# Hybrid decoder layer: the depthwise convolution as three filters by parity of tokens, its norm's sums in float32r of rounded values and rests

## The reference, cut to what matters

```python
u = conv_val * jax.nn.sigmoid(conv_gate)
u = causal_depthwise_conv(u, conv_w[layer], conv_b[layer])      # width 31, 512 channels
uf = u.astype(jnp.float32).reshape(B, S, N_CONV_GROUPS, CONV_GROUP_DIM)   # 4 groups of 128
mu_c = jnp.mean(uf, axis=-1, keepdims=True)
var_c = jnp.mean(jnp.square(uf - mu_c), axis=-1, keepdims=True)
uf = ((uf - mu_c) * lax.rsqrt(var_c + EPS)).reshape(B, S, D_CONV)
uf = uf * conv_norm_w[layer].astype(jnp.float32) + conv_norm_b[layer].astype(jnp.float32)
y_conv = jax.nn.silu(uf).astype(x.dtype)
```

## Time and profile before

| | |
|---|---|
| time, median of 3 runs | 2086.36 us (2085.43 to 2087.7) |
| the profiled execution's own time | 2085.33 us |
| its span, first to last instruction | 2083.5 us |
| TensorE busy | 2067.1 us (99%) |
| VectorE busy | 1446.1 us (69%) |
| ScalarE busy | 912.1 us (44%) |
| mean granted TensorE clock | 0.998 |

### The profile page before, as it was taken

The page is one execution under the profiler, slowest core; times in us unless marked ns, Lnnn a source line. Parts: engine busy times, 40 slices in busy tenths (PEclk is TensorE's granted clock), DMA queues, the critical chain, the costliest instruction groups (busy, mean ns, idle before and its releaser), DMA issues. The chain is left out here.

```text
span 2083.5 us, 26901 instructions
## 1 busy us (share of the span) xinstructions
PE 2067.1 (99%) x10031; PEld 1734.2 (83%) x10031; DVE 1446.1 (69%) x1993; ACT 912.1 (44%) x1557; POOL 417.2 (20%) x252
## 2 busy tenths in 40 slices
PE   9999999999999999999999999999999999999998
PEld 8897878878788888788888888888788888888887
DVE  6897999989567777886666976666563536624285
ACT  6632434343454445754555654455331313313163
POOL 0000000000002323352332333232353134400012
PEclk9999999999999999999999999999999999999999
DMA  5121212113656875765446755545756455543376
GB/s 204 32 87 47 70 41 81 51 32 105 199 177 195 266 235 171 266 192 167 137 142 191 236 171 156 167 150 189 245 210 259 154 193 202 174 169 126 138 257 218
DMA packets 254144, 338.55 MB, mean 162 GB/s; under 512 B 11584, under 2 KB 195648, under 8 KB 240192
## 3 DMA queue, kind: packets, MB, share of 16 engines
q1 hardware_dynamic: 221376, 315.80, 45.6%
q10 hardware_dynamic: 32384, 20.98, 3.2%
q0 software_dynamic: 256, 0.07, 0.0%
HBM read 225.58 MB, written 111.21 MB: 162 GB/s over the span
## 5 line engine op out<-in xcount | busy, mean ns | idle before, releaser
L1978 PE MATMUL psum<-x_hi,w_hi_P 128*128 128x512 f32 x896 | 349.8, 390 | 3.8 <-DVE x_lo L1922 2.4
L2198 PE MATMUL psum<-w_hi,hid_hi 128*128 128x512 f32 x896 | 348.8, 389 | 1.9 <-DVE hid_lo L2074 1.9
L1978 PE MATMUL psum<-x_lo,w_hi_P 128*128 128x512 f32 x896 | 349.1, 390 | 0.0
L1978 PE MATMUL psum<-x_hi,w_lo_P 128*128 128x512 f32 x896 | 349.1, 390 | 0.0
L2198 PE MATMUL psum<-w_hi,hid_lo 128*128 128x512 f32 x896 | 348.6, 389 | 0.0
L2198 PE MATMUL psum<-w_lo,hid_hi 128*128 128x512 f32 x896 | 348.6, 389 | 0.0
L2074 DVE TENSOR_TENSOR hid_lo<-hid_raw,hid_hi 128x1024 fp32r<-128x1024 f32 x112 | 174.4, 1593 | 211.4 <-ACT hid_hi L2069 211.4
L1891 POOL TENSOR_TENSOR w_raw<-w_raw 128x512 f32<-128x512 f32 x128 | 184.9, 1467 | 395.3 <-DVE w_lo_P L1904 345.8
L2069 ACT ACTIVATE hid_hi<-hid_raw 128x1024 fp32r<-128x1024 f32 x112 | 112.9, 1051 | 343.4 <-DMA hid_raw<-scratch_hid 343.3
L1904 DVE TENSOR_TENSOR w_lo_P<-w_raw,w_hi_P 128x512 fp32r<-128x512 f32 x224 | 184.1, 834 | 98.1 <-ACT w_hi_P L1900 95.5
L1900 ACT ACTIVATE w_hi_P<-w_raw 128x512 fp32r<-128x512 f32 x224 | 136.0, 626 | 236.8 <-PE psum L1978 227.2
(11 more groups left out here) (284 smaller groups left out, 3820.0 us busy)
## 6 DMA issues: line engine op xcount, KB each, us to landing
scratch_hid<-stage SPq DMA_DIRECT2D x224, 256.0 KB, 3.7
hid_raw<-scratch_hid SPq DMA_DIRECT2D x56, 1024.0 KB, 4.9
w_raw<-in_w SPq DMA_DIRECT2D x52, 1024.0 KB, 5.0
w_grain<-in_w SPq DMA_DIRECT2D x48, 512.0 KB, 5.3
x_raw<-scratch_h2s SPq DMA_DIRECT2D x14, 1024.0 KB, 8.4
w_raw<-in_w_in SPq DMA_DIRECT2D x22, 512.0 KB, 3.6
scratch_h2s<-h2s SPq DMA_DIRECT2D x8, 1280.0 KB, 10.1
scratch_qk<-qout ACTq DMA_DIRECT2D x16, 512.0 KB, 3.3
```

Of the source, the lines that this page charges most:

```text
L1978: mm = nc.tensor.matmul(psum[:, bank_1(op, g), :], l, r, start=kt == 0 and i == 0, stop=kt == 3 and i == 2)
L2198: mm = nc.tensor.matmul(psum[:, bank, :], l, r, start=f == 0 and k == 0, stop=f == NFP - 1 and k == 2)
```

## The change

Tokens are stored by parity: `u_buf` holds a unit's even and odd tokens in two halves, each with its own head. Three filters of half the length run over 512 or 513 pairs each: A (the 16 even taps over the one half), B (the 15 odd taps over the other), and M (sums of neighbouring taps over sums of neighbouring tokens, `u_pairs`). Even outputs are A + B, odd ones are M minus (A shifted + B). A unit is `N_STEPS` = 48 steps on VectorE: S (the token sums), 15 A, 14 B, 15 M, E, T and O. ScalarE makes the first product of each filter (`first_taps`, `pair_tap`), and in its loop these stand ahead of `silu_qk` and `first_tap_qk`. `SILU` puts the tokens back in order as it writes.

For the norm, ScalarE rounds `c_buf` to float32r (`HIGH`), VectorE makes the rest (`LOW`), and the sums are float32r matmuls of both; the squares are treated alike (`HIGH` of the square on ScalarE, `SQUARE_LOW` on VectorE). The rounded values lie in the unit's own place in `u_buf`, so `glu` of the unit that comes to that place now waits for all six counts of `ln_sum`, that is for `VAR` and no longer for the last tap.

```diff
-AT_MEAN, AT_CENTER, AT_SQUARE, AT_VAR, AT_RSTD, AT_NORM, AT_SILU = 1, 2, 3, 4, 5, 6, 7
-LAST_UNIT_AT = {AT_MEAN: 0, AT_CENTER: 0, AT_SQUARE: 0, AT_VAR: 1, AT_RSTD: 1, AT_NORM: 1, AT_SILU: 1}
+UNIT_AT = {AT_HIGH: 0, AT_SUM_HIGH: 1, AT_LOW: 1, AT_SUM_LOW: 2, AT_CENTER: 2, AT_SQUARE: 3, AT_SQUARE_LOW: 3,
+           AT_VAR: 5, AT_RSTD: 6, AT_NORM: 7, AT_SILU: 8}
+LAST_UNIT_AT = {AT_HIGH: 0, AT_SUM_HIGH: 1, AT_LOW: 1, AT_SUM_LOW: 2, AT_CENTER: 2, AT_SQUARE: 2, AT_SQUARE_LOW: 2,
+                AT_VAR: 3, AT_RSTD: 3, AT_NORM: 3, AT_SILU: 3}
-TAP_COST = 23
+STEP_COST = 12.6
...
+def unit_steps():
+    out = [("S", 0)]
+    for j in range(1, EVEN):
+        out += [("A", j)] + ([("B", j)] if j < ODD else []) + ([("M", j - 1)] if j > 1 else [])
+    return out + [("E", 0), ("M", EVEN - 1), ("T", 0), ("O", 0)]
...
-                    for b in range(2):
-                        group_sum(c_buf[:, u % 2], b)
+                    for b in range(2):
+                        group_sum(high_part(u), b, True, False).then_inc(sem["ln_sum"], 1)
+                for u in units_at(s, AT_SUM_LOW):
+                    pe.wait_ge(sem["ln_dve"], 3 * u + 1)
+                    for b in range(2):
+                        group_sum(high_part(u), b, False, True).then_inc(sem["ln_sum"], 1)
                 for u in units_at(s, AT_VAR):
-                    pe.wait_ge(sem["c_sq"], u + 1)
+                    pe.wait_ge(sem["ln_act"], 3 * u + 3)
+                    pe.wait_ge(sem["ln_dve"], 3 * u + 3)
                     for b in range(2):
-                        group_sum(rstd, b)
+                        group_sum(high_part(u), b, True, False)
+                        group_sum(square_low, b, False, True).then_inc(sem["ln_sum"], 1)
...
+                for u in units_at(s, AT_HIGH):
+                    act.wait_ge(sem["tap"], step_done(u, "O"))
+                    nc.scalar.activation(high_part(u), c_buf[:, u % 2], ACT.Copy).then_inc(sem["ln_act"], 1)
...
+                for u in range(N_UNITS):
+                    if FIRST_TAP[u] == s:
+                        first_taps(u)
+                    if PAIR_TAP[u] == s:
+                        pair_tap(u)
                 for j, half in convs_at(s - 2):
                     silu_qk(j, half)
                 for j, half in convs_at(s):
                     first_tap_qk(j, half)
-                for u in range(N_UNITS):
-                    if FIRST_TAP[u] == s:
-                        first_tap(u)
-                    if SECOND_TAP[u] == s:
-                        second_tap(u)
...
                 if tb % 2 == 0 and u >= U_RING:
-                    dve.wait_ge(sem["tap"], DVE_TAPS * (u - U_RING + 1))
+                    dve.wait_ge(sem["ln_sum"], LN_SUMS * (u - U_RING + 1))
...
+                nc.vector.scalar_tensor_tensor(out=a_sum, in0=u_halves(u)[:, 0, j:j + UH + 1],
+                                               scalar=par[:, CONV_W + g * CW + 2 * j:CONV_W + g * CW + 2 * j + 1],
+                                               in1=a_sum, op0=ALU.mult, op1=ALU.add).then_inc(sem["tap"], 1)
...
                 for j, half in convs_at(s - 1):
                     convolve_qk(j, half)
+                for u in units_at(s, AT_LOW):
+                    dve.wait_ge(sem["ln_sum"], LN_SUMS * u + 2)
+                    nc.vector.tensor_tensor(high_part(u), c_buf[:, u % 2], high_part(u).bitcast(F32),
+                                            ALU.subtract).then_inc(sem["ln_dve"], 1)
...
+                for u in units_at(s, AT_SQUARE_LOW):
+                    dve.wait_ge(sem["ln_act"], 3 * u + 3)
+                    nc.vector.tensor_tensor(square_low[:], rstd[:], high_part(u).bitcast(F32),
+                                            ALU.subtract).then_inc(sem["ln_dve"], 1)
```

More of the change, by code:

```diff
@@ L498, in slot, with group_sum @@
                 mm.then_inc(sem["proj"], 1)
-            def group_sum(src, b):
-                nc.tensor.matmul(psum[:, 6 + b, :], ones[:], src[:, b * TB:(b + 1) * TB],
-                                 start=True, stop=True).then_inc(sem["ln_sum"], 1)
+            def group_sum(src, b, start, stop):
+                return nc.tensor.matmul(psum[:, 6 + b, :], ones_r[:], src[:, b * TB:(b + 1) * TB], start=start, stop=stop)
             scores, numerators, transpose_y = tail["tensor"](pe)[:3]
@@ L513, in tensor @@
                 slot(s)
-                for u in units_at(s, AT_MEAN):
-                    pe.wait_ge(sem["tap"], DVE_TAPS * (u + 1))
+                for u in units_at(s, AT_SUM_HIGH):
+                    pe.wait_ge(sem["ln_act"], 3 * u + 1)
                     if u == 0:
@@ new lines, in odd_tap @@
+            def odd_tap(u, j):
+                g = u // 2
+                if j == 1:
+                    dve.wait_ge(sem["tap0"], 3 * u + 2)
+                else:
+                    dve.wait_ge(sem["tap"], step_done(u, "B", j - 1))
+                nc.vector.scalar_tensor_tensor(out=b_sum, in0=u_halves(u)[:, 1, j:j + UH],
+                                               scalar=par[:, CONV_W + g * CW + 2 * j + 1:CONV_W + g * CW + 2 * j + 2],
+                                               in1=b_sum, op0=ALU.mult, op1=ALU.add).then_inc(sem["tap"], 1)
@@ new lines, in even_tokens, with both_sums, odd_tokens @@
+            def even_tokens(u):
+                dve.wait_ge(sem["tap"], step_done(u, "A", EVEN - 1))
+                nc.vector.tensor_tensor(c_buf[:, u % 2, 0:UH], a_sum[:, 0:UH], b_sum, ALU.add).then_inc(sem["tap"], 1)
+            def both_sums(u):
+                dve.wait_ge(sem["tap"], step_done(u, "E"))
+                nc.vector.tensor_tensor(b_sum, a_sum[:, 1:UH + 1], b_sum, ALU.add).then_inc(sem["tap"], 1)
+            def odd_tokens(u):
+                dve.wait_ge(sem["tap"], step_done(u, "T"))
+                nc.vector.tensor_tensor(m_sum(u), m_sum(u), b_sum, ALU.subtract).then_inc(sem["tap"], 1)
@@ new lines, in conv_step @@
+            def conv_step(n):
+                u = n // N_STEPS
+                kind, j = STEPS[n % N_STEPS]
+                if kind == "S":
+                    add_pairs(u)
+                elif kind == "A":
+                    even_tap(u, j)
+                elif kind == "B":
+                    odd_tap(u, j)
+                elif kind == "M":
+                    pair_tap(u, j)
+                elif kind == "E":
+                    even_tokens(u)
+                elif kind == "T":
+                    both_sums(u)
+                else:
+                    odd_tokens(u)
@@ new lines, in add_weights @@
+            def add_weights():
+                taps = par[:, CONV_W:CONV_W + H * CW].rearrange("p (g k) -> p g k", g=H)
+                sums = pairs[:, 0:H * EVEN].rearrange("p (g j) -> p g j", g=H)
+                nc.vector.tensor_tensor(sums[:, :, 0:ODD], taps[:, :, 0:CW - 1:2], taps[:, :, 1:CW - 1:2], ALU.add)
+                nc.vector.tensor_copy(sums[:, :, ODD:EVEN], taps[:, :, CW - 1:CW])
+                link(nc.vector.tensor_scalar(pairs[:, H * EVEN:H * EVEN + H], par[:, CONV_B:CONV_B + H], 2.0, None, ALU.mult))
```

165 lines of the change are left out of this document (107 added, 58 removed).

## The result

The changed kernel takes **2104.36 us** (median of 4 runs, 2103.3 to 2107.08) against 2086.56 for the kernel before (2085.43 to 2087.7): ratio 1.0088, 95% interval 1.0076 to 1.01. It is slower by 17.8 us; I had forecast slower by 7. The profiled execution took 2103.3.

The account below looks back on a forecast made before the run. TensorE was taken as the bound, busy 2067.1 of 2083.5 us. Terms -13.1 - 1.9 + 0.7 + 2.7 + 0.7 + 6.4 + 8.0 + 3.4 = +6.9 gave 2092.2 profiled, 2093 forecast, range 2080 to 2098.

Parts of the forecast that it names:

- main case: Long TensorE pauses both at unit 6 and at the tail: slower, 2093 us, own range 2089 to 2097; chance 0.52.
- Sums, -13.1: On TensorE, eight float32r matmuls a unit replace two pairs of float32 sums: -13.1 us over eight units.
- waits that go, -1.9: TensorE's waits for the convolution's mean (1.1 us) and slot 91's wait for an evacuation (0.78) vanish: -1.9 us.
- VectorE at 0.66 us a step: On VectorE, each filter step over 512 tokens takes 0.66 us, 48 steps making 31.7 us a unit.
- rival (5): VectorE's steps cost more than 0.66 us (0.74), so deadlines are missed in each unit: 2103 us; chance 0.08.
- Units 2, 3 and 6: TensorE waits for HIGH or LOW at these units: +0.7, +2.7 (0.9 and 1.8), and +0.7 with +6.4 us.
- Units 0, 1, 4 and 5 ... nothing there: HIGH of these units has 1 to 5 us left before TensorE needs it, so no wait was charged.
- The chain behind VAR is the same. +8.0: At the tail, TensorE waits for yc_c at scores(0), only slot 91 lying between: +8.0 us, bounds 6.5 and 8.5.
- I charge each the same: +3.4: Half clock on TensorE behind the 6.4 and 8.0 us pauses, 1.7 us lost each: +3.4 us, bounds 0 and 6.
- (2): Only the tail pause comes, LOW of unit 6 waiting for little: 2085 us; chance 0.17.
- (3): Only unit 6's pause comes, yc_c no longer being last: 2088 us at best, 2083 if all goes; chance 0.1.
- (4): Neither the pause at unit 6 nor that at the tail comes: 2075 us, faster; chance 0.13.

Follow-up runs that it names:

- last mended kernel: The four edits of the mended kernels, plus eight of unit 7's steps in VectorE's slot 80 with LOW of unit 6 ahead of them: 2077.91 us.
- mended kernels: Changed kernel with LOW ahead of q/k block, slot 55's silu ahead of RSTD, own buffer for unit 6's tokens, float32 sums for unit 7: 2085.97 us.
- hand-made pause of 7.96 us: Kernel before, with TensorE's means of units 4 and 5 made to wait for three and six more taps: 2099.13 us, 1.0061.
- loads by half: Changed kernel with own buffers for tokens of units 6 and 7, first eight chunks' yc_c loads waiting only for first-half units: 2101.41 us, 1.0069.

## Why the prediction was wrong in size

The sign and the main case (pauses at unit 6 and at the tail) were right. The forecast for the profiled execution was 2092.2; it took 2103.3, 11.1 more. By its terms:

- **Sums, -13.1, and waits that go, -1.9:** held as far as seen: the sum for the last mended kernel comes out with 11.4 for seven units and 1.1 of the waits, and the 0.78 at slot 91 is gone from the changed kernel's waits (it is back where unit 7's sums are float32).
- **VectorE at 0.66 us a step:** held. VectorE's timeline around a glu, and the later glu that waits for VAR of unit 2:

```profile
271.54 0.68 DVE L902 SCALAR_TENSOR_TENSOR u_buf<-th,psum 128x512 f32<-128x512 f32 x1
272.14 0.75 DVE L933 SCALAR_TENSOR_TENSOR c_buf<-u_pairs,pair_weights,c_buf 128x512 f32<-128x512 f32 x1
272.80 0.75 DVE L912 SCALAR_TENSOR_TENSOR ab_buf<-u_buf,par_a,ab_buf 128x513 f32<-128x513 f32 x1
...
289.72 0.18 DVE L895 COPY u_buf<-u_buf 128x30 f32<-128x30 f32 x1 [7.47 <-PE psum L556]
```

  Steps start 0.66 apart, and `glu` with strides takes 0.68 as before, so nothing was the right price for it and rival (5), steps above 0.70, is out.
- **Units 2, 3 and 6:** forecast 0.7, 0.9 + 1.8, 0.7 + 6.4; measured 0.76, 0.91 + 1.85, 1.04 + 5.88. (The terms written out for unit 2 add to 9.5, not 9.7, which makes its wait 0.5.) The glu of slot 45 waits 7.47 us for VAR of unit 2, as said. LOW ahead of the block showed that the q/k block was the cause.
- **"Units 0, 1, 4 and 5 ... nothing there": wrong for unit 4**, 3.25. I counted steps and left out ScalarE's order: RSTD one slot later meets the silu of block (5, 0). Shown by the move of that silu, in slot 55 alone in the mended kernels: the wait for HIGH is 0.50 there. A wait of 1.27 for LOW then shows, so even with the silu in place "nothing there" was 1.8 us short. That part was not tested; as at unit 2, VectorE has S, seven steps and here a weight split too (1.14) between O and LOW.
- **"The chain behind VAR is the same. +8.0": mis-sized, 9.55 (4.49 + 5.06), above its bounds.** I priced the chain behind VAR and left the one ahead of it at nothing. SQUARE waits for unit 6's DMA. Behind VAR, `scores(0)` starts after 13.3 us (567.36 to 580.67), 1.1 less than my 14.4, and slot 91 itself took longer at the lower clock, so this part was 5.06. With SQUARE's wait gone the pause behind VAR was 7.15, within my bounds of 6.5 to 8.5.
- **The clock, "I charge each the same: +3.4": mis-sized, 8.4, above its bounds of 0 and 6.** There were four long pauses (3.25 to 5.88 us) and not two, and behind them 1.7 to 2.9 us was lost, not 1.7 each. The Trainium skill (TensorE: Matmul & The Clock Gate, HAM oscillation) says that idle stretches put TensorE back to half clock; the hand-made pause of 7.96 us agrees, with 2.1 us lost behind it, while behind that of 1.65 the clock stayed at 1.00.
- **The rest, 1.4**, had no term.

Pauses 4.7, clock 5.0 and the rest 1.4 make the 11.1. Rivals (2), (3) and (4) each need one or both pauses to be absent; both were there. (Rival (4) takes off 16 for the two pauses and their clock, where the terms are 6.4 + 8.0 + 3.4 = 17.8; its time would be 2074.)

## What to carry over

When a step of a fixed order is moved by a slot, look on every engine at what it now stands ahead of, above all where that neighbour feeds a chain with a DMA in it; here the wait showed up on TensorE 27 us and one unit later, under another name. A pause of TensorE costs its length and, where the clock falls behind it, more: in the profiled executions each pause of 3.24 to 7.96 us was followed by half clock, and 1.5 to 3.0 us went with it. Cheaper matmuls pay only if the order around them gives back what the new passes ask: here nearly the same sums (unit 7's float32 again) were worth -8 us or +18 by where five things stood, and taking pauses away one by one showed the next one each time.

## What the runs showed of the hardware

Whether the clock falls behind a short pause, and for how long it stays low behind a long one, differed between executions with the same pause:

- Behind 1.85 us (unit 3) it stayed at 1.00 in the profiled runs of the changed kernel (322 to 330 us) and of the tail with float32 sums (321 to 326), and fell in four others; with the silu moved it read 0.76 from 322 to 326 and 0.81 to 330, behind 1.86.
- Behind 2.4 us (unit 2) it stayed at 1.00 with the silu moved (2.45; 275 to 281 us) and fell with the first products last (2.43; 0.50 from 274 to 276).
- Behind 3.25 us (unit 4) 1.5 us were lost with unit 6's tokens in their own buffer (0.63 over 4.0 us) and 2.8 with the loads by half (0.50 over 5.5 us).

Of these, the kernels with unit 6's tokens in their own buffer, with the loads by half and with the float32 tail differ from the changed kernel only at the tail, so up to unit 6 they are the same program. This may be why the changed kernel's runs lie further apart (3.8 us against 2.3 for the kernel before); it was not tested.
